# A fused stick-breaking and HGRN2 block: late HGRN2 steps one point later, and waits moved at the start and in the gate phase

## The reference

```
h    = rmsnorm(x) ; proj = h @ w_in            # columns: sb_q sb_k sb_v sb_z | hg_q hg_f hg_i hg_z | 2048 gate logits
sb   = stick-breaking attention(sb_q, sb_k, sb_v)       # strictly causal, per head
hg_o = HGRN2(silu(hg_q), 1-f, log f, hg_i)              # S_t = diag(f_t) S_{t-1} + k_t v_t^T ; o_t = S_t^T q_t
hg_o = rmsnorm over each head's 128 values
u_sb = (sb * silu(sb_z)) @ w_sb_proj ; u_hg = (hg_o * silu(hg_z)) @ w_hg_proj
y    = sigmoid(gate_sb) * u_sb + sigmoid(gate_hg) * u_hg
out  = rmsnorm(x + y @ w_out)
```

## Time and profile before

| | |
|---|---|
| median of three runs | 1359.74 us (1359.3 to 1360.8) |
| profiled execution | 1358.94 us, span 1357.2 us |
| granted TensorE clock, mean | 0.997 |
| busy: PE, PEld | 1329.0 us (98%), 1108.9 us (82%) |
| busy: DVE, ACT, POOL | 903.1 us (67%), 549.4 us (40%), 709.5 us (52%) |
| one head, from one step 6 to the next | 112.68 us |

### The profile page before, as it was taken

One profiled execution on the slowest core, in us unless ns is written; L12 is line 12 of the kernel. 1 busy time (PEld: TensorE's weight loads), 2 busy tenths in 40 slices (PEclk: granted clock), 3 DMA queues, 4 the chain that ended last, 5 costly groups with the idle time before them and its releaser, 6 DMA issues.

```text
span 1357.2 us, 22985 instructions
## 1 busy us (share of the span) xinstructions
PE 1329.0 (98%) x8393; PEld 1108.9 (82%) x8393; DVE 903.1 (67%) x1076; ACT 549.4 (40%) x899; POOL 709.5 (52%) x475
## 2 busy tenths in 40 slices
PE   8899999999999999999999999999999999999998
PEld 6788788788878878878888887887887888888886
DVE  5838877877877887787687788778635455645223
ACT  7543355255345335524534533552444431111121
POOL 5655564654665556455466556645578722223310
PEclk9999999999999999999999999999999999999999
DMA  5122111211112211121111211113543485434502
GB/s 187 31 62 65 47 62 32 82 58 46 62 46 73 66 32 62 31 92 56 37 62 46 77 62 31 62 31 118 176 180 133 155 266 191 124 93 132 202 27 98
DMA packets 128168, 118.55 MB, mean 87 GB/s; under 512 B 3920, under 2 KB 110464, under 8 KB 128128
## 3 DMA queue, kind: packets, MB, share of 16 engines
q1 hardware_dynamic: 118816, 92.81, 21.5%
q10 hardware_dynamic: 9312, 25.19, 5.4%
HBM read 88.63 MB, written 29.36 MB: 87 GB/s over the span
## 4 chain that ended last, share of the span: by engine, by line
PE 82%; DVE 7%; issue 5%; POOL 2%; ACT 2%; DMA 1%; ACTq 0%; DVEq 0%; SPq 0%; POOLq 0%
PE banks L1693 44%; PE banks L1986 13%; PE banks L2030 7%; PE banks L1773 5%; PE banks L1751 4%; PE banks L1763 2%; DVE hk L1176 2%; DVE forget L1176 2%; DVE scT L1422 1%; PE banks L1832 1%; PE banks L1737 1%; PE banks L1807 1%; POOL b_lo L631 1%; POOL b_sum L631 1%; PE banks L1834 1%
## 5 line engine op out<-in xcount | busy, mean ns | idle before, releaser
L1693 PE MATMUL banks<-a_hi,b_hi 128*128 128x512 f32 x1064 | 432.7, 407 | 6.4 <-issue 3.8
L1693 PE MATMUL banks<-a_hi,b_lo 128*128 128x512 f32 x1064 | 417.1, 392 | 0.0
L1693 PE MATMUL banks<-a_lo,b_hi 128*128 128x512 f32 x1064 | 415.7, 391 | 0.0
L631 POOL TENSOR_TENSOR b_lo<-w_raw,b_hi 128x512 fp32r<-128x512 f32 x106 | 162.2, 1540 | 231.9 <-ACT b_hi L733 231.9
L631 POOL TENSOR_TENSOR b_lo<-b_sum,b_hi 128x512 fp32r<-128x512 f32 x114 | 167.7, 1471 | 148.2 <-ACT b_hi L733 148.2
L1693 PEld LDWEIGHTS banks<-a_hi,b_hi 128*128 128x128 f32 x1064 | 200.3, 188 | 46.1 <-issue 7.5
L1693 PEld LDWEIGHTS banks<-a_hi,b_lo 128*128 128x128 f32 x1064 | 199.9, 188 | 44.3
L1693 PEld LDWEIGHTS banks<-a_lo,b_hi 128*128 128x128 f32 x1064 | 200.8, 189 | 35.9
L733 ACT ACTIVATE b_hi<-b_sum 128x512 fp32r<-128x512 f32 x114 | 72.0, 632 | 152.5 <-POOL b_sum L631 151.9
L717 POOL TENSOR_TENSOR w_lo<-w_raw,w_hi 128x1024 fp32r<-128x1024 f32 x20 | 54.5, 2730 | 133.5 <-ACT w_hi L733 133.5
L631 POOL TENSOR_TENSOR b_sum<-w_raw 128x512 f32<-128x512 f32 x68 | 102.9, 1513 | 0.0
(11 more groups left out here) (219 smaller groups left out, 2564.8 us busy)
## 6 DMA issues: line engine op xcount, KB each, us to landing
w_raw<-in_w_in SPq DMA_DIRECT2D x72, 512.0 KB, 4.9
gate_d<-gate_out SPq DMA_DIRECT2D x16, 512.0 KB, 4.6
gate_in<-gate_d ACTq DMA_DIRECT2D x32, 256.0 KB, 2.7
x_tok<-in_x SPq DMA_DIRECT2D x8, 512.0 KB, 6.6
z_d<-z_out SPq DMA_DIRECT2D x8, 512.0 KB, 2.7
hz_d<-z_out SPq DMA_DIRECT2D x8, 512.0 KB, 2.7
osb_d<-o_sb SPq DMA_DIRECT2D x8, 512.0 KB, 5.7
ohg_d<-hq SPq DMA_DIRECT2D x8, 512.0 KB, 2.7
```

Source lines behind the costliest of these rows:

```text
L631: return nc.gpsimd.tensor_tensor(dst, a, b, op)
L1693: last = mm(bank, w[:, s, k, :], t[s][:, k, :], start=opens and k == 0 and z == 0, stop=k == QUAD - 1 and z == 2, skip_group_check=not opens)
```

## The change

1. `HG_AT`: steps 6, 7, 8, 9, 11 and 12 go from behind points 14, 17, 19, 21, 23 and 26 to behind points 15, 18, 20, 22, 24 and 27. PE's and ACT's orders change, DVE's doesn't.
2. At the start the wait for all four sums is taken out. In its place each product of the third pair whose operand is such a sum waits for its own (and those made before it), and ACT waits for the last before it writes head 0's second sigmoid, whose buffer the last sum is still read from.
3. In the gate phase DVE multiplies the second gated tile of a pair (tile 3 at g = 4) after C22 instead of ahead of u3, its low part comes after C12, and ACT makes its high part at point 10 instead of 7.

```diff
+SUM_OPERANDS = (P7, P6, P5, P3)
...
-HG_AT = {1: 0, 3: 1, 6: 3, 9: 4, 12: 5, 14: 6, 17: 7, 19: 8, 21: 9, 23: 11, 26: 12}
+HG_AT = {1: 0, 3: 1, 6: 3, 9: 4, 12: 5, 15: 6, 18: 7, 20: 8, 22: 9, 24: 11, 27: 12}
...
             def sigmoids(h, j):
                 act.wait_ge(qk_done, 8 * h + j + 1)
+                if isinstance(h, int) and h == 0 and j == 1:
+                    act.wait_ge(s_ready, 4)
...
-                    if p == 7 and not final:
-                        for e in OSB_GATED.get(g, ()):
+                    if p in (7, 10) and not final:
+                        for e in OSB_GATED.get(g, ())[:1] if p == 7 else OSB_GATED.get(g, ())[1:]:
                             osb_high(e)
...
                 take_u2(n, n)
-                for e in OSB_GATED.get(g, ())[:1 if last_pair else None]:
+                for e in OSB_GATED.get(g, ())[:1]:
                     osb_gate(e)
                 take_u3(n, n)
...
                 if not last_pair:
                     for e in OSB_TIMES_Z[g][1:]:
                         osb_multiply(e)
-                for e in OSB_GATED.get(g, ())[:1 if last_pair else None]:
+                    for e in OSB_GATED.get(g, ())[1:]:
+                        osb_gate(e)
+                for e in OSB_GATED.get(g, ())[:1]:
                     osb_low(e)
...
                 if last_pair:
                     for e in OSB_GATED[g][1:]:
                         osb_gate(e)
-                    for e in OSB_GATED[g][1:]:
-                        osb_low(e)
+                for e in OSB_GATED.get(g, ())[1:]:
+                    osb_low(e)
...
                 if p % 2 == 0:
                     product_waits(n, s)
+                    if isinstance(n, int) and n == 2 and s in SUM_OPERANDS:
+                        pe.wait_ge(s_ready, max(SUM_OPERANDS.index(t) for t in SUM_OPERANDS if t <= s) + 1)
...
             pe.wait_ge(p1_copied, 2)
             pe.wait_ge(first_taken, 2)
-            pe.wait_ge(s_ready, 4)
             pe.wait_ge(const_made, CONSTANTS)
             second_half(0)
```

## The result

The changed kernel takes **1383.97 us** (median of four runs, 1383.07 to 1384.10) against 1359.52 for the kernel before (four runs, 1358.74 to 1360.80): a ratio of 1.0178, 95% interval 1.016 to 1.0195. It is slower, as forecast, but by 24.4 us and not by the 14.7 of the prediction, and outside its range of 1368 to 1379. The profiled execution took 1384.1 us with a span of 1382.4 and a mean granted clock of 0.992.

What follows compares the result with a forecast made beforehand. The prediction took PE's instruction stream, with few holes, to bound the kernel. 1358.94 - 3.7 (start) + 14.7 (loop) + 3.7 (gate phase) + 0 (gate order) = 1373.6; with 0.8 for the runs' median, 1374.4 us, range 1368 to 1379.

Steps and rivals of the forecast that it cites:

- the mechanism of edit 1 in the loop: In each of seven heads P3 waits 2.1 us for C22, then the turned values wait 1.4 us for v_diff.
- the bound of 0.7 a head: Lower bound for a head's loss in the loop, 0.7 us, if v_diff weren't in the way.
- only v_diff's wait takes the place of step 6's: Rival for the loop: P3's wait ends in time, the loop gives 0, the kernel takes 1357.7 us; chance 0.03.
- edit 2: At the start, the third pair's wait for the sums and its half clock go: -3.7 us, bounds 0 and -5.5.
- edit 3: In the gate phase, 1.8 us less wait at g = 4 is given back two pairs later: 0.
- the gate phase: Last head, gate pairs 0 and 1: late outputs and ACT's order make PE 3.7 us late, bounds 0.7 and 4.6.
- its part by the sigmoid: Gate pair 1: the large gate sigmoid now stands ahead of the root on ACT, about 1.6 us.
- The sum: Whole kernel: -3.7 at the start, +14.7 in the loop, +3.7 in the gate phase, 0 for the gate order.
- The clock falls in the new waits: Rival for the waits in the heads: 1.7 us lost once in each of eight heads, +13.6, 1388 us; chance 0.07.
- the loop's own term: Seven heads of the loop, each later from the turned values on: +14.7 us.
- 2.1 for a head: Loop: v_diff, and everything from the turned values on, comes 2.1 us later in each head.
- "Nothing" for ACT's order: Loop: ACT's weight splits of points 15, 20 and 24 moving ahead of copies and squares cost nothing.

Runs made afterwards that it cites:

- C22 first: The changed kernel with DVE taking C22 of the second pair ahead of the carry of the states, in the loop and gate pair 1: 1362.61 us, 1.0019.
- v_diff first: The changed kernel with DVE taking C21 and making v_diff ahead of the first reciprocal, C22 left where the change has it: 1369.72 us, 1.0073.

## Why the prediction was right and wrong

**Right: the mechanism of edit 1 in the loop.** P3 waits for C22 behind the carry (2.1 forecast, 2.0 measured), then the turned values for v_diff (1.4 and 1.65), and the second fixes the period, not the first. Taking either alone away shows it: with C22 first the period is still 113.45, with v_diff first 113.4 in the heads without a fall (the bound of 0.7 a head), and only with both 111.8. The case "only v_diff's wait takes the place of step 6's", priced at 1357.7, was even built: C22 first and ACT's old order took 1357.54, with step 6's wait closed, v_diff's at 1.3, and the period that of before.

**Right: edit 2** (-3.7 forecast, -4.0 alone), **edit 3** (0 and 0), **the gate phase** (+3.7 and +3.8 without its fall of the clock), its part by the sigmoid shown by 2.1 us given back. The start's -4.0 holds in the changed kernel too: 3.8 from x_tok to the first turn.

**Wrong: the clock.** The sum has no term for the clock in the new waits. The step that failed is the one that put it at nothing: the rival "The clock falls in the new waits", given 0.07 and left outside the range, and its argument that "today's waits of 1.3 and 2.2 leave the mean clock at 0.997". In its place the runs showed six falls of 1.6 us behind waits of 2.0. They make 9.6 of the 10.5 us by which the profiled span's difference (25.2) is above the sum's (14.7); the loop's own term adds 1.4, the gate phase 0.1, and the start takes 0.8 back. The price of one fall, 1.7, was right. Two errors stand in the argument. A mean over the span can't speak of one wait, since a fall moves it by about 0.001; and a single wait of 2.2 that kept the clock is one case, which fell the other way when the steps alone were moved. Besides, the rival was priced as all or nothing, eight falls and 1388, where some heads and not others was open too. The page of the Trainium skill that the prediction cites there (TensorE: Matmul & The Clock Gate, "Why this matters for your kernels") names gaps longer than either new wait, so it didn't bear out the rival; here the measured falls decide.

**Too small: 2.1 for a head.** It is 2.3. "Nothing" for ACT's order is the step that missed it: the splits that come ahead of the copies let POOL run into DVE's instructions. In head 3 of the changed kernel, without a fall, DVE's timeline has:

```profile
397.13 0.29 DVE L1440 COPY hk<-banks 128x128 f32<-128x128 f32 x1
...
413.55 1.52 DVE L1181 TENSOR_TENSOR v_diff<-turn_in 128x1023 f32<-128x1023 f32 x1
414.99 0.14 DVE L1329 COPY v_diff<-turn_in 128x1 f32<-128x1 f32 x1
```

The outputs, at 401.89, start 4.76 us behind the carry, and before 2.65: 2.1 later, as forecast. From there to v_diff's end it takes 13.24 us and not 13.04, 0.2 more. In the changed kernel DVE's idle time ahead of the carry, 2.08 us before and now gone, takes up k_lo's and q_lo's part, and v_diff's 0.3 is left; with C22 in that place too it was 0.76. This mis-sized term is 1.4 us over seven heads. The 0.76 is shown by a run; the 0.2 of the changed kernel is read from its rows, no run has its order with ACT's old table alone.

**Open: which heads lose the clock.** In the profiled executions of all kernels the clock never fell in the loop with a wait of at most 1.7 us, and it fell in 20 of 35 heads with a wait of 2.0 or 2.4 for z_out. Every such fall starts between 0.3 us ahead of that wait's end and 1.3 us behind it. Three kernels with the same periods lost it in the same heads, 1, 2, 4, 5 and 7, so it isn't mere chance; but equal waits in equal surroundings did or did not cost it, and the longer wait did so less often. The number of falls isn't fixed for a kernel either: with v_diff first the four executions have mean clocks of 0.993 to 0.996, and one fall is 0.001. So the two falls of its profiled execution, the fastest and the one of 0.996, may be the fewest. Nor does the length alone hold outside the loop: at the start, where PE stands more often, six of the profiled executions show a fall at about 12 us, 1.4 to 2.0 us behind a wait of 1.5 to 1.8 us for x_tok. The Trainium skill (TensorE: Matmul & The Clock Gate, "Why this matters for your kernels") warns of long gaps between bursts of matmuls; a rule by the gap's length alone doesn't tell heads 2 and 3 apart. That the falls come from z_out's wait is shown by taking it away; what picks the head isn't.

## What to carry to other kernels

A step that is put later to close a wait on one engine must be followed through the order of the other engines: here the work that covered C22 and v_diff was the same point that was moved, and with edits 2 and 3 in both, moving only step 6 gave -12.8 us where moving all six steps cost 24. Count a new wait of some 2 us on PE as its length plus the chance of a stretch at half clock (here 20 in 35, 1.6 us each), and look for that in the windows right behind waits of the kernel before, not in the mean. When ACT's order changes, look at what POOL and DVE then do at the same time.

## What the runs showed of the hardware

- A wait of 2.0 or 2.4 us on PE can be followed by 3.4 us of granted clock 0.50, a loss of 1.6 us; waits of 1.2 to 1.7 us in the loop never were, also not in the 21 heads of three kernels that had no longer wait. At the start waits of 1.5 to 1.8 us were, in six profiled executions.
- DVE instructions with two SBUF inputs and POOL's tensor operations lengthen each other: the later one by the overlap less about 0.15 us, up to 0.97 us of 1.12. An edit that moves only ACT's splits was worth 0.76 us a head by this.
- A wait that the list puts on POOL's b_lo (1.98 us in gate pair 1) vanished when DVE's C22 came earlier, and with C22 0.4 us later the list puts it on DVE's gate_out (2.4 us): of several semaphores the list names one.
